# Expert rows added in DRAM: residual rows stored first, the experts' gated rows added by accumulating scatters that take turns

## What is computed

```python
x = x + mix @ w_out                                  # x1 in the kernel, 1152 x 1024
h = rmsnorm(x, g_ffn)                                # h2
# each token: group g (top 1 of 4), then its two best of the 8 experts of the group
gate = softmax(e_val) * p_top                        # 2 gates per token
out[tok] = sum over j of gate[j] * (silu(h @ w_gate[e_j]) * (h @ w_up[e_j])) @ w_down[e_j]
x = x + out
y = rmsnorm(x, g_final)
```

## Time and profile before

| | |
|---|---|
| time, median of 3 runs | 1238.06 us (1234.52 to 1239.92) |
| the profiled execution: time | 1236.26 us |
| its span | 1234.4 us |
| TensorE's granted clock, mean of the span | 0.969 of full speed |
| PE busy | 1129.7 us |
| DVE busy | 848.8 us |
| ACT busy | 686.9 us |
| POOL busy | 229.5 us |
| DMA | 205.35 MB |

### The profile page before, as it was taken

How to read it: one execution, slowest core, us unless ns; L and a number is a source line. 1 busy time by engine, 2 the same in 40 slices (tenths; PEclk the granted TensorE clock), 3 DMA queues, 4 the chain that set the end, 5 groups by cost and what they waited for, 6 DMA issues and landing times.

```text
span 1234.4 us, 18077 instructions
## 1 busy us (share of the span) xinstructions
PE 1129.7 (92%) x6469; PEld 928.9 (75%) x6469; DVE 848.8 (69%) x1760; ACT 686.9 (56%) x1187; POOL 229.5 (19%) x275
## 2 busy tenths in 40 slices
PE   5997799999999999999999889996899999999954
PEld 5984478787878888888988578885588888888831
DVE  6528878888888776443232642446799999999945
ACT  6347578686878233343433531122388888887822
POOL 1320023334343100000000000000133333433111
PEclk8999999999999899999999999998899999999978
DMA  8352030404030242432423743003799999999656
GB/s 283 44 109 37 31 99 1 111 2 111 1 88 1 59 120 73 112 97 78 118 61 93 240 127 160 35 35 137 270 412 406 391 391 391 400 387 391 260 228 263
DMA packets 129552, 205.35 MB, mean 166 GB/s; under 512 B 17412, under 2 KB 102820, under 8 KB 117172
## 3 DMA queue, kind: packets, MB, share of 16 engines
q1 hardware_dynamic: 114868, 177.61, 41.4%
q0 software_dynamic: 12864, 21.02, 5.5%
q10 hardware_dynamic: 1728, 5.51, 1.1%
HBM read 182.02 MB, written 34.37 MB: 175 GB/s over the span
## 4 chain that ended last, share of the span: by engine, by line
PE 78%; DVE 10%; DMA 4%; ACT 4%; issue 3%; POOL 0%; SPq 0%; DVEq 0%; POOLq 0%; ACTq 0%
PE psum L2573 5%; PE psum L2571 5%; PE psum L2572 5%; PE psum L2278 5%; PE psum L2280 5%; PE psum L2279 4%; DVE place L1503 3%; PE psum L2431 3%; PE psum L2429 3%; PE psum L2430 3%; PE psum L2250 3%; PE psum L2252 2%; PE psum L2251 2%; PE psum L2590 2%; PE psum L2525 2%
## 5 line engine op out<-in xcount | busy, mean ns | idle before, releaser
L1941 DVE TENSOR_TENSOR place<-place,place 128x2048 fp32r<-128x2048 f32 x62 | 141.7, 2287 | 10.5 <-ACT place L1296 9.9
L1111 ACT ACTIVATE place<-place,place 128x768 uint8<-128x768 f32 (+3 forms) x128 | 125.5, 984 | 6.7 <-DVE place L1534 6.7
L2278 PE MATMUL psum<-place,place 128*128 128x512 f32 x288 | 121.9, 423 | 2.4 <-DVE place L1491 2.4
L1296 ACT CAST place<-place 128x2048 fp32r<-128x2048 f32 x62 | 118.5, 1915 | 0.0
L2280 PE MATMUL psum<-place,place 128*128 128x512 f32 x288 | 113.4, 394 | 0.0
L2279 PE MATMUL psum<-place,place 128*128 128x512 f32 x288 | 112.6, 391 | 0.0
L2571 PE MATMUL psum<-place,place 128*128 128x512 f32 x248 | 102.7, 414 | 0.0
L2573 PE MATMUL psum<-place,place 128*128 128x512 f32 x248 | 97.9, 395 | 0.0
L2572 PE MATMUL psum<-place,place 128*128 128x512 f32 x248 | 97.3, 392 | 0.0
L2250 PE MATMUL psum<-place,place 128*128 128x256 f32 x288 | 86.9, 302 | 3.5 <-ACT place L1133 3.5
L2251 PE MATMUL psum<-place,place 128*128 128x256 f32 x288 | 82.9, 288 | 0.0
(11 more groups left out here) (336 smaller groups left out, 3092.4 us busy)
## 6 DMA issues: line engine op xcount, KB each, us to landing
place<-in_w_gate SPq DMA_DIRECT2D x32, 1024.0 KB
place<-in_w_up SPq DMA_DIRECT2D x32, 1024.0 KB
place<-in_w_down SPq DMA_DIRECT2D x32, 1024.0 KB, 10.7
place<-in_w_in SPq DMA_DIRECT2D x28, 512.0 KB, 6.2
place<-expert_out SPq DMA_DIRECT2D x9, 1024.0 KB, 14.3
place<-in_cache_attn_k SPq DMA_DIRECT2D x32, 256.0 KB, 3.2
place<-in_cache_attn_v SPq DMA_DIRECT2D x32, 256.0 KB, 3.5
place<-in_x_prompt SPq DMA_DIRECT2D x3, 1536.0 KB, 6.9
```

Source lines behind the costliest of these rows:

```text
L1111: last = nc.scalar.activation(reached[j], score[j], ACT.Sign, bias=pivot.bitcast(F32)[:, j:j + 1], scale=-1.0, accum_out=minus[:, j - BY_A ...
L1296: nc.scalar.copy(w_gu_hi[e % 2][:, :, ks, :], w_gu[e % 3][:, :, ks, :]).then_inc(w_hi_done, 1)
L1941: nc.vector.tensor_tensor(w_gu_lo[e % 3][:, :, ks, :], w_gu[e % 3][:, :, ks, :], w_gu_hi[e % 2][:, :, ks, :].bitcast(F32), ALU.subtract).t ...
L2278: nc.tensor.matmul(bank(4 + b), hT_hi[:, k, rows], hi, start=k == 0, stop=False)
```

## The change

x1's tiles are stored to a new DRAM tensor, summed_rows (1152 x 1024), by SP behind each store of h2. The down product's rows are multiplied by their gate when they leave PSUM, the scale being a column, slot_gates; the column comes from a wider product in `over_frames` (68 columns instead of 18, fp32 instead of fp32r), ahead of which DVE computes four more small operations. The scatters go to summed_rows at the token's index, and they add (compute_op=ALU.add). Since both rows of a token go to the same row of DRAM, each scatter waits until the one before has landed, the first until x1 is stored. The last stage loads one row per token, 512 KB a tile, straight into x1, and only norms it; the sums on DVE and PE are gone, and so is PE's part of the stage. The scaling that DVE did (L2063) is done by POOL, and the stores follow the squares by three tiles. block_rows, expert_out, y_in and the gate diagonals are gone; frames_done counts 3 instead of 5. The diff, cut to its core (memory places, semaphore names, changed counts of frames_done and the index copies of the overflow loop are left out; "..." stands between hunks):

```diff
@@ -801,11 +794,13 @@
                 sp.dma_start(h2_dram[t * P:(t + 1) * P, :], h2[t % 2]).then_inc(h2_out[t % 2], 16)
+                sp.dma_start(summed_rows[t * P:(t + 1) * P, :], x1[:, t, :]).then_inc(x1_out, 16)
             sp.dma_start(h2_dram[TP * P:, :], h2[TP % 2]).then_inc(h2_out[TP % 2], 16)
+            sp.dma_start(summed_rows[TP * P:, :], x1[:, TP, :]).then_inc(x1_out, 16)
...
@@ -844,7 +839,7 @@
             for t in range(T):
-                sp.dma_start(y_in[t], expert_out.rearrange("(j t p) d -> t p j d", j=2, p=P)[t]).then_inc(y_loaded(t)[0], 16)
+                sp.dma_start(x1[:, t, :], summed_rows[t * P:(t + 1) * P, :]).then_inc(y_loaded(t)[0], 16)
...
@@ -933,19 +928,24 @@
                 pool.wait_ge(y_dve, e + 1)
-                pool.indirect_dma_start(expert_out, bass.IndirectOffsetOnAxis(ap=block_rows[:, e:e + 1], axis=0), y_rows[e % 2], None,
-                                        bounds_check=2 * NTOK - 1, oob_is_err=False).then_inc(y_out[e % 2], 16)
+                if e:
+                    pool.wait_ge(y_out[(e - 1) % 2], 16 * ((e + 1) // 2))
+                else:
+                    pool.wait_ge(x1_out, 16 * T)
+                pool.indirect_dma_start(summed_rows, bass.IndirectOffsetOnAxis(ap=block_frames[:, e:e + 1], axis=0), y_rows[e % 2], None,
+                                        bounds_check=NTOK - 1, oob_is_err=False, compute_op=ALU.add).then_inc(y_out[e % 2], 16)
             gather(1)
-            pool.wait_ge(frames_done, 2)
-            pool.wait_ge(frames_done, 5)
+            pool.wait_ge(frames_done, 3)
+            pool.wait_ge(y_out[0], 16 * NE // 2)
+            pool.wait_ge(y_out[1], 16 * NE // 2)
...
@@ -962,12 +962,14 @@
                         stand(pool)
-                        pool.indirect_dma_start(expert_out, bass.IndirectOffsetOnAxis(ap=rows_now, axis=0), y_rows[0], None,
-                                                bounds_check=2 * NTOK - 1, oob_is_err=False).then_inc(over_out, 16)
+                        pool.indirect_dma_start(summed_rows, bass.IndirectOffsetOnAxis(ap=frames_now, axis=0), y_rows[0], None,
+                                                bounds_check=NTOK - 1, oob_is_err=False, compute_op=ALU.add).then_inc(over_out, 16)
             for t in range(T):
+                pool.wait_ge(ssq_done, 2 * T + t + 1)
+                pool.tensor_scalar(ssq7[:, t:t + 1], ssq7[:, t:t + 1], 1.0 / D, EPS, ALU.mult, ALU.add).then_inc(ms_done, 1)
...
@@ -1312,18 +1314,18 @@
                 if e == 0:
-                    act.wait_ge(frames_done, 3)
+                    act.wait_ge(frames_done, 2)
                 if e == 0:
-                    act.wait_ge(frames_done, 5)
+                    act.wait_ge(frames_done, 3)
                     act.wait_ge(y_out[e % 2], 16 * (e // 2))
-                nc.scalar.copy(y_rows[e % 2][:, 0:512], bank(down_bank(e))).then_inc(y_act, 1)
+                nc.scalar.activation(y_rows[e % 2][:, 0:512], bank(down_bank(e)), ACT.Copy, scale=slot_gates[:, e:e + 1]).then_inc(y_act, 1)
...
@@ -1354,9 +1356,6 @@
             rows_out(NE - 1)
-            for n, t in enumerate(ON_PE):
-                for j in range(2):
-                    nc.scalar.activation(gate_diagonal[n][j], ident, ACT.Copy, scale=gates[:, j, t:t + 1]).then_inc(mix_hi_done, 1)
...
@@ -1368,24 +1367,19 @@
                         act.wait_ge(y_out[0], 16 * NE // 2)
-                        nc.scalar.copy(y_rows[0][:, 0:512], bank(6)).then_inc(y_act, 1)
+                        act.wait_ge(over_now, 2 * i + 2)
+                        nc.scalar.activation(y_rows[0][:, 0:512], bank(6), ACT.Copy, scale=gate_now).then_inc(y_act, 1)
             y_p, y_s = o_["y_p"].rearrange("a s d -> (a s) d"), o_["y_s"].rearrange("b s d -> (b s) d")
-            for x in range(T + 1):
+            for x in range(T + 3):
                 if x < T:
-                    t = LAST_ORDER[x]
-                    if t in ON_PE:
-                        act.wait_ge(wo_ps, T + ON_PE.index(t) + 1)
-                        rows = bank(2 * ON_PE.index(t), 0, D)
-                    else:
-                        act.wait_ge(x2_done, x2_after(x))
-                        rows = x1[:, t, :]
+                    act.wait_ge(*y_loaded(x))
                     act.wait_ge(ssq_done, 2 * T + x)
-                    nc.scalar.activation(squared, rows, ACT.Square, accum_out=ssq7[:, x:x + 1]).then_inc(ssq_done, 1)
-                if x >= 1:
-                    t = LAST_ORDER[x - 1]
-                    act.wait_ge(out_done, x)
-                    act.dma_start(y_p[t * P:(t + 1) * P, :] if t < TP else y_s, out_rows[t]).then_inc(y7_out[(x - 1) % 3], 16)
+                    nc.scalar.activation(squared, x1[:, x, :], ACT.Square, accum_out=ssq7[:, x:x + 1]).then_inc(ssq_done, 1)
+                if x >= 3:
+                    t = x - 3
+                    act.wait_ge(out_done, t + 1)
+                    act.dma_start(y_p[t * P:(t + 1) * P, :] if t < TP else y_s, x1[:, t, :]).then_inc(y7_out[t % 3], 16)
...
@@ -1960,7 +1953,7 @@
                     v.wait_ge(y_out[e % 2], 16 * (e // 2))
-                nc.vector.tensor_scalar(y_rows[e % 2][:, 512:D], bank(down_bank(e) + 1), 1.0, None, ALU.mult).then_inc(y_dve, 1)
+                nc.vector.tensor_scalar(y_rows[e % 2][:, 512:D], bank(down_bank(e) + 1), slot_gates[:, e:e + 1], None, ALU.mult).then_inc(y_dve, 1)
...
@@ -1996,7 +1989,13 @@
                 over_blocks = C("blocks")[:, NE:NBLK].unsqueeze(1).unsqueeze(1).broadcast_to([P, 2, T, NOVER])
-                tt(at_over, slot_block.unsqueeze(3).broadcast_to([P, 2, T, NOVER]), over_blocks, ALU.is_equal).then_inc(slots_done, 1)
+                share_of_row = slots_f
+                L(v, nc.vector.reciprocal(share_of_row, C("row").rearrange("p (j t) -> p j t", j=2)))
+                L(v, tt(share_of_row, share_of_row, gates, ALU.mult))
+                L(v, tt(over_sums[:, :, :, 0:NOVER], slot_block.unsqueeze(3).broadcast_to([P, 2, T, NOVER]), over_blocks, ALU.is_equal))
+                L(v, tt(over_sums[:, :, :, NOVER:NOVER + NE], hot_pe.bitcast(F32), share_of_row.unsqueeze(3).broadcast_to([P, 2, T, NE]), ALU.mult))
+                tt(over_sums[:, :, :, NOVER + NE:], over_sums[:, :, :, 0:NOVER], share_of_row.unsqueeze(3).broadcast_to([P, 2, T, NOVER]),
+                   ALU.mult).then_inc(slots_done, 1)
...
@@ -2005,7 +2004,8 @@
                 v.wait_ge(frames_ps, len(PARTS) + 1)
-                place_frames(slice(NE, NBLK), bank(5, 0, NOVER)).then_inc(frames_done, 1)
+                L(v, nc.vector.tensor_copy(slot_gates, bank(5, NOVER, NBLK)))
+                place_frames(slice(NE, NBLK), bank(5, 0, NOVER))
...
@@ -2043,24 +2043,13 @@
                         v.wait_ge(y_out[0], 16 * NE // 2)
-                        nc.vector.tensor_scalar(y_rows[0][:, 512:D], bank(7), 1.0, None, ALU.mult).then_inc(y_dve, 1)
+                        v.wait_ge(over_now, 2 * i + 2)
+                        nc.vector.tensor_scalar(y_rows[0][:, 512:D], bank(7), gate_now, None, ALU.mult).then_inc(y_dve, 1)
             v.wait_ge(g_final_in, 16)
-            for x in range(T + 1):
-                if x < T and LAST_ORDER[x] not in ON_PE:
-                    t = LAST_ORDER[x]
-                    v.wait_ge(*y_loaded(t))
-                    for j in range(2):
-                        nc.vector.scalar_tensor_tensor(x1[:, t, :], y_in[t][:, j, :], gates[:, j, t:t + 1], x1[:, t, :], ALU.mult, ALU.add).then_inc(x2_done, 1)
-                        v.wait_ge(x2_done, x2_after(x) - 1 + j)
-                if x >= 1:
-                    t = LAST_ORDER[x - 1]
-                    v.wait_ge(rstd_done, 2 * T + x)
-                    rows = bank(2 * ON_PE.index(t), 0, D) if t in ON_PE else x1[:, t, :]
-                    nc.vector.scalar_tensor_tensor(out_rows[t], rows, rstd7[:, x - 1:x], g_final, ALU.mult, ALU.mult).then_inc(out_done, 1)
-                if x < T:
-                    v.wait_ge(ssq_done, 2 * T + x + 1)
-                    nc.vector.tensor_scalar(ssq7[:, x:x + 1], ssq7[:, x:x + 1], 1.0 / D, EPS, ALU.mult, ALU.add).then_inc(ms_done, 1)
+            for t in range(T):
+                v.wait_ge(rstd_done, 2 * T + t + 1)
+                nc.vector.scalar_tensor_tensor(x1[:, t, :], x1[:, t, :], rstd7[:, t:t + 1], g_final, ALU.mult, ALU.mult).then_inc(out_done, 1)
...
@@ -2517,7 +2506,7 @@
                     for t in range(T):
-                        last = nc.tensor.matmul(bank(5, 0, NOVER), at_row(j, t), at_over[:, j, t, :], start=j == t == 0, stop=j == 1 and t == T - 1)
+                        last = nc.tensor.matmul(bank(5, 0, NGATE), at_row(j, t).bitcast(F32), over_sums[:, j, t, :], start=j == t == 0, stop=j == 1 and t == T - 1)
...
@@ -2629,15 +2618,6 @@
-            pe.wait_ge(mix_hi_done, T + 2 * len(ON_PE))
-            for n, t in enumerate(ON_PE):
-                pe.wait_ge(*y_loaded(t))
-                for m in range(2):
```

(38 more changed lines are left out.)

3 lines of the change are left out of this document (1 added, 2 removed).

## The result

The changed kernel takes 1258.13 us as a median (1253.87 to 1259.84, four executions) against 1237.98 for the kernel before, measured beside it: a ratio of 1.0172 with an interval of 1.0149 to 1.0195. It is 20 us slower. The forecast was 1228, a gain; the first rival, "the turn becomes the bound", had 1255.

The account below looks back on a forecast made before the run. PE bound 32 experts at 9.52 us, DMA the first 30 us of a 47.4 us tail. Tail -16.9, last scatters +2.2, lateness +4.8 made -9.9 from 1236.26: 1226.4, plus 1.8, so 1228 us; range 1219 to 1262.

Parts of the forecast that it names:

- Rival 1: Expert stage, POOL's wait for the scatter before: landing 10.0 us makes turns bind, net +17, 1255 us; chance 0.23.
- a turn is then 7.8 + 1.2 + 0.84 = 9.84: Expert stage: a scatter's median landing, 1.2 for adding and 0.84 restart make a turn 0.32 us over PE's pace.
- the formula: Expert stage's lateness for a scatter landing L: 27 x (L - 8.68) - 3.9 us, at least 0; forecast +4.8.
- Room for the plain scatter: Expert stage: pace 9.52 less restart 0.84 less median landing 7.8 leaves 0.88 us per scatter.
- Net effect of everything but lateness: Whole kernel without late expert turns: tail 16.9 us less, last two scatters 2.2 us more, net -14.7 us.
- Tail: Last stage from the first load's issue: 47.4 us falls to 30.5, with tiles at a cadence c of 2.05 us.
- The slack of 3.9 us: Expert stage: gathers are issued early enough that 3.9 us of scatter lateness is used up before PE is late.
- the 2.2 for the last scatters in turn: End of the expert stage: the last two scatters take turns, 2.2 us more, between 0.7 and 5.
- The stage ahead of the experts: Before the experts: x1 stores, DVE's small operations and the wider overflow product are covered, 0; the product at most 0.5 us.
- Its hard form: Expert stage: engines finish one row before the next, 1 us more per row, landing 12.3, about 1317 us; chance 0.10.
- Rival 2: Expert stage: DMA bandwidth capped at 393 GB/s, 10.27 us per expert, net +1.6, 1240 us; chance 0.22 together with Rival 3.
- Rival 3: Expert stage or tail: landing near 9.3 or slower tail and last scatters cancel the gain; chance 0.22 together with Rival 2.

Follow-up runs that it names:

- kernel 1: The changed kernel with experts in the order 0, 8, 16, 24, 1, ... and no wait for the scatter before: 1226.59 us, ratio 0.9911 to the kernel before.
- kernel 7: kernel 1 with the tail's scaling of the sum of squares moved from POOL to DVE, one tile ahead of its product: 1223.21 us, ratio 0.9884.
- kernel 6: The changed kernel with each gather issued one scatter earlier on POOL: 1238.31 us, ratio 1.0007 to the kernel before.
- kernel 2: kernel 1 with each scatter's wait for the one before put back: 1252.57 us, ratio 1.0123 to the kernel before.
- kernel 5: The changed kernel with each of DVE's 2048-column subtractions cut into four of 512 columns: 1257.57 us, ratio 1.0171 to the kernel before.
- kernel 4: The kernel before with only the wait of each scatter for the one before added, scatters plain: 1237.77 us, ratio 1.0006.
- kernel 3: The changed kernel with scatters that write in place of adding, still in turn: 1221.82 us, ratio 0.9869 to the kernel before.

## Why the prediction was wrong, and where it was right

**The step that failed** is "a turn is then 7.8 + 1.2 + 0.84 = 9.84". The turn is 11.11. Mechanism, place and formula were in the forecast, as its first rival; its term for what adding costs a landing was mis-sized: 1.2 where it is 11.11 - 0.84 - 7.8 = 2.5. Of that the runs show two pieces.

First, the bytes. The queue that carries gathers and scatters shows them (packets, MB, share of 16 engines' span); the kernel before, then the kernel after:

```profile
q0 software_dynamic: 12864, 21.02, 5.5%
```
```profile
q0 software_dynamic: 12864, 21.03, 7.3%
```

The packets and the MB are the same, the time isn't: 7.3% of 1257.9 less 5.5% of 1234.4 is 23.9 us, 0.75 for each of 32 scatters. In the traces, a row's packet of 4 KB keeps an engine for 0.16 us in a gather or a plain scatter and for 0.33 in an adding scatter; 4.5 rows per engine make 0.75 as well. The forecast's lower bound, 0.7, was the price of the data, and it was right.

Second, POOL. The prediction gave POOL's own 1.00 us per scatter no increase, and the landing is counted from its start. The groups of instructions by line (busy us, mean ns) of before and of after:

```profile
L936 POOL DMA_INDIRECT expert_out<-place,place x32 | 32.1, 1004 | 192.3 <-DVE place L1963 186.3
```
```profile
L935 POOL DMA_INDIRECT summed_rows<-place,place x32 | 76.9, 2403 | 217.3 <-DMA summed_rows<-place,place 155.1
```

1.40 us more in the mean. 0.59 of it belongs to adding as such: every adding scatter of kernel 1 takes 1.55 to 1.64. The other 0.8 comes where scatters are held back by the turn. The sum 7.8 + 0.75 + POOL's increase gives 9.1 for kernel 7, 9.9 for the change and 9.6 for kernel 6 with its mean of 2.05; the mean landings of scatters 0 to 26 are 9.2, 10.2 and 9.4. It accounts for the size within 0.3 us. The packets agree: the first row of a scatter moves 5.5 us after the scatter's start in the change and 4.4 in kernels 1 and 7, so what a held-back scatter loses, it loses before its first row.

The median of the page, 9.9, would have misled even after the fact: with it a turn is 10.7 and not 11.11. It takes in the five landings without load. Over the 27 turns mean (10.2) and median (10.5) are both higher.

Even with 1.4 in place of 1.2, the price of a scatter that waits for none (9.2 - 7.8), the formula gives 27 x (9.2 - 8.68) - 3.9 = 10.1, 1233 us. That would have been near the forecast. **The turn makes its own landings longer:** kernels 1 and 2 differ by the wait alone, and with it scatters stay on POOL for up to 3.46 us where none stays over 1.64 without; their mean landing is 10.0, where that of free ones is 9.2 (kernel 7). The forecast's argument was the opposite, that a slower PE thins out the weight loads and shortens L; DMA did fall from 393 to 346 GB/s, and L rose.

**What stays open:** why POOL is kept up to 3.6 us by a scatter that starts late, and why that is rarer with gathers further ahead. Shorter instructions on DVE (kernel 5) didn't change it. Other engines' accesses at that moment, and the phase against the weight loads, weren't tried apart.

**Point by point.** Room for the plain scatter, 0.88 us: right (kernel 4). Net effect of everything but lateness, -14.7 us: -14.6 (kernel 3), but that it agrees so well is luck. By the spans it is 1220.5 - 1234.4 = -13.9 us. In kernel 3 the tail from the first load's issue (1189.42) is 31.1 us and not 30.5, the last scatters add 0.2 (1189.42 - 1155.40 = 34.0 for 33.8) and not 2.2, and scatter 27 starts 2.2 us later than before, since experts come every 9.63 us and not 9.52; the forecast put that at nothing, and no run shows where it comes from. Tail, 30.5 us (28.1 to 33.3): 28.55; c = 2.05 was 2.00, and the rest is 0.9 less to the first product (5.6 us for 6.45) and 0.7 less behind the last. The slack of 3.9 us and the 2.2 for the last scatters in turn, -1.7 together: -0.7 measured. The stage ahead of the experts: covered, but for the overflow product. The forecast let it cost at most 0.5; the chain of after has it at

```profile
886.48 3.97 PE psum L2509 x36
```

where before it was 2.07. The duration of one, 0.11 us, was right and their number wrong: an fp32 product of 68 columns is two such instructions here. The forecast had taken it from what it called eight fp32 matmuls of 128 columns; those are transposes (L2525), and each is one instruction. Of these 1.9 us, 0.8 show in scatter 1's start (906.76 against 905.97 before).

**The rivals.** Rival 1 had 1255 at L = 10.0; the measured turn less 0.84, 10.27, gives 27 x 1.59 - 3.9 - 14.7 = +24.3, and the spans differ by 23.5: the tail was 2.0 better, the small terms 1.0 worse, and the rest is rounding. The medians differ by 20.2, since the profiled execution of before lies 1.7 us below its median and that of after 1.7 above. Its hard form (1317) did not come: it had each row cost 1 us more, 4.5 us in all, and the shortest adding landing, without traffic, is 5.0 us where the plain one is 2.7. Rival 2, bandwidth, came to 1240 and is refuted by kernel 1: 27 adding scatters at a pace of (1159.51 - 895.70) / 27 = 9.77 us against (1155.40 - 895.38) / 27 = 9.63 for plain ones in kernel 3. It had 10.27. With the second read counted, (3.74 + 0.295) MB in 9.77 us are 413 GB/s, an estimate, since the profile's bytes leave that read out; the 393 GB/s weren't all the engines can do. What adding without a wait costs at all is the 4.8 us of experiment 3. The Trainium skill, "Collectives: The Full Stack", section "The bandwidth ceiling: the fold count and why AG ≠ RS ≠ AR", has the adding step of a ring collective move at about half the rate of a copy, by its two read descriptors per chunk. This trace agrees, though it is no collective: 0.33 us of engine time per row in place of 0.16. As a forecast of this kernel's time the rule would have mattered little, since what decides is how long one transfer takes and who waits for it. Rival 3 (L near 9.3) describes kernel 6.

## What to carry to other kernels

Where a change makes transfers wait for one another, the landing of each turns from something hidden into a link of the chain. Its room is the pace less the landing less the restart (here 9.52 - 7.8 - 0.84), and once the room is used up each turn costs the full difference, 27 times here; a price of 1.2 us that is wrong by 1.3 decides the sign. Take the landings from the stretch in which they will be links, not from all of them (10.2 against 9.9 here), and let a held-back transfer be dearer than a free one (10.0 to 10.2 against 9.2). Where the view of waits names a producer, check against the landing and the restart whether it was not the transfer after all. Before accepting such a wait, look for an order of the work in which neighbours don't conflict: the same bytes, with experts of different groups in succession and no wait, are 26.0 us faster than with the wait in the same order, 31.5 us faster than the change (on another chip) and 0.9% faster than the kernel before; with the tail's scaling moved from POOL to DVE it is 1.2%, which the intervals don't tell from 0.9.

## What the runs showed of the hardware

- An adding scatter of 0.295 MB keeps POOL for 1.55 to 1.64 us where a plain one takes 1.00, before any wait, and its landing without other traffic is 4.7 to 5.0 us where a plain one's is 2.7.
- The same instruction, held back by the wait for the scatter before, kept POOL for up to 3.62 us (3.74 in kernel 5).
- A row of 4 KB keeps a DMA engine for 0.16 us in a gather or a plain scatter and for 0.33 in an adding one; the profile's packets and bytes are the same for both.
- From the landing of one scatter to the start of the next on POOL it is 0.87 us where POOL waits for it.
- An operation of POOL on one column took 0.18 us alone and 1.28 us when it began beside DVE's product of 1024 columns, ending with it; this sets the cadence of the tail.
- An fp32 product of 68 columns shows as two instructions, 0.11 us apart.
